# Strassen's scheme in the output projection of a hybrid attention block: chunks 2 and 3 of 4 by seven half-size products for eight

## The reference

```python
mixed = jax.nn.sigmoid(g_sb) * y_sb + jax.nn.sigmoid(g_sa) * y_sa
h = h + jnp.einsum('bsd,de->bse', mixed, w_out[layer])     # (512 x 2048) by (2048 x 2048)
return rms_norm(h, final_norm_gain)
```

## Time and profile before

| | |
|---|---|
| median of three runs | 1643.45 us |
| the profiled execution's own time | 1644.75 us |
| its span (first to last instruction) | 1643.1 us |
| TensorE matmul busy | 1628.2 us, 99% |
| TensorE weight load busy | 1357.3 us, 83% |
| VectorE busy | 754.4 us, 46% |
| ScalarE busy | 580.9 us, 35% |
| GpSimd busy | 16.2 us, 1% |
| moved by DMA | 165.90 MB, mean 101 GB/s |
| granted TensorE clock, mean | 0.998 of full |

### The profile page before, as it was taken

One profiled execution on the slowest core, in us unless ns is written; L12 is line 12 of the kernel. 1 busy time (PEld: TensorE's weight loads), 2 busy tenths in 40 slices (PEclk: granted clock), 3 DMA queues, 4 the chain that ended last, 5 costly groups with the idle time before them and its releaser, 6 DMA issues.

```text
span 1643.1 us, 20351 instructions
## 1 busy us (share of the span) xinstructions
PE 1628.2 (99%) x7443; PEld 1357.3 (83%) x7443; DVE 754.4 (46%) x1116; ACT 580.9 (35%) x926; POOL 16.2 (1%) x37
## 2 busy tenths in 40 slices
PE   8999999999999999999999999999999999999998
PEld 6888888888888888888888888888888888888886
DVE  5334678622125444354544554444455544434333
ACT  5333333222225454344443233333233433313222
POOL 0000000000000000000000000000000000000000
PEclk9999999999999999999999999999999999999999
DMA  5232233333333322233323333323232523253233
GB/s 195 78 100 79 79 89 90 102 89 91 103 102 91 96 83 83 83 98 88 96 77 103 105 93 96 93 85 95 83 102 83 185 90 103 90 202 121 94 106 115
DMA packets 82043, 165.90 MB, mean 101 GB/s; under 512 B 7104, under 2 KB 7632, under 8 KB 80848
## 3 DMA queue, kind: packets, MB, share of 16 engines
q1 hardware_dynamic: 77808, 150.10, 30.1%
q0 software_dynamic: 3040, 13.63, 2.2%
q10 hardware_dynamic: 1152, 1.57, 0.3%
HBM read 156.90 MB, written 8.39 MB: 101 GB/s over the span
## 4 chain that ended last, share of the span: by engine, by line
PE 98%; DMA 0%; DVE 0%; ACT 0%; issue 0%; SPq 0%; DVEq 0%
PE proj L1098 28%; PE proj L1099 28%; PE proj L1100 28%; PE attn L1099 3%; PE attn L1100 3%; PE attn L1098 3%; PE attn L1259 1%; PE attn L1288 1%; PE attn L1220 1%; PE attn L1219 1%; PE attn L1146 0%; DMA xs<-in_x 0%; PE proj L1166 0%; PE attn L1261 0%; DVE xs L738 0%
## 5 line engine op out<-in xcount | busy, mean ns | idle before, releaser
L1098 PE MATMUL proj<-u_hi,w_hi 128*128 128x512 f32 x1536 | 600.9, 391 | 2.5 <-DVE xs L738 2.5
L1099 PE MATMUL proj<-u_lo,w_hi 128*128 128x512 f32 x1536 | 598.7, 390 | 0.0
L1100 PE MATMUL proj<-u_hi,w_lo 128*128 128x512 f32 x1536 | 598.7, 390 | 0.0
L683 DVE TENSOR_TENSOR w_lo<-stage,w_hi 128x1024 fp32r<-128x1024 f32 x267 | 325.9, 1223 | 518.1 <-ACT w_hi L369 515.5
L369 ACT ACTIVATE w_hi<-stage 128x1024 fp32r<-128x1024 f32 x267 | 282.0, 1060 | 484.6 <-PE proj L1100 356.7
L1098 PEld LDWEIGHTS proj<-u_hi,w_hi 128*128 128x128 f32 x1536 | 288.9, 188 | 61.8 <-DVE xs L738 2.8
L1100 PEld LDWEIGHTS proj<-u_hi,w_lo 128*128 128x128 f32 x1536 | 288.7, 188 | 60.4
L1099 PEld LDWEIGHTS proj<-u_lo,w_hi 128*128 128x128 f32 x1536 | 288.9, 188 | 58.4
L385 ACT ACTIVATE area<-proj 128x512 f32 (+1 forms) x80 | 47.9, 599 | 171.3 <-PE proj L1100 171.2
L1098 PE MATMUL proj<-w_hi,u_hi 128*128 128x512 f32 x256 | 99.9, 390 | 0.0
L1100 PE MATMUL proj<-w_hi,u_lo 128*128 128x512 f32 x256 | 99.6, 389 | 0.0
(11 more groups left out here) (177 smaller groups left out, 1419.9 us busy)
## 6 DMA issues: line engine op xcount, KB each, us to landing
stage<-in_w_in SPq DMA_DIRECT2D x208, 512.0 KB, 3.7
stage<-in_w_out SPq DMA_DIRECT2D x32, 512.0 KB, 3.6
stage<-in_w_branch_sb SPq DMA_DIRECT2D x16, 512.0 KB, 3.6
stage<-in_w_branch_sa SPq DMA_DIRECT2D x16, 512.0 KB, 4.0
xs<-in_x SPq DMA_DIRECT2D x4, 1024.0 KB, 8.7
o_scratch<-og POOLq DMA_DIRECT2D x16, 256.0 KB, 2.3
hres<-in_x POOLq DMA_DIRECT2D x1, 4096.0 KB, 13.6
o_in<-o_scratch POOLq DMA_DIRECT2D x3, 1024.0 KB, 6.1
```

Of the source, the lines that this page charges most:

```text
L683: V.tensor_tensor(w_lo[:, s % RING, :, :], stage[:, s % 2, :, :], w_hi[:, s % RING, :, :].bitcast(F), ALU.subtract).then_inc(strip_lo, 1)
L1098: nc.tensor.matmul(out_, a_hi, b_hi, start=start, stop=False, skip_group_check=free)
L1099: nc.tensor.matmul(out_, a_hi, b_lo, start=False, stop=False, skip_group_check=free)
L1100: return nc.tensor.matmul(out_, a_lo, b_hi, start=False, stop=stop, skip_group_check=free)
```

## The change

Chunk 30 stays as it was. Chunks 31 and 32 are computed by the Strassen-Winograd scheme. Tokens are halved (256 and 256), W's K tiles are split into even and odd ones, and the 512 columns into two of 256 (`HW`). Seven products of half size replace eight. A unit of this work is a form strip q = 0 to 15 (eight for each chunk); it holds seven forms of a pair of K tiles, each 128 x 256: B11, B22, B21 and the sums S1 to S4. TensorE runs 7 products x 2 token tiles x 3 = 42 matmuls of 256 moving columns per form strip (`form_strip`).

- SP's queue issues three loads for each form strip into one of four `raw` buffers. Two of them write their source twice, so that S1 and S3 begin as copies.
- GpSimd's queue then adds the missing block to S1 and S3 by a DMA that accumulates (16 of them, line 433 of the new file).
- VectorE adds S2 and S4 (`form_sums`), ScalarE writes the high parts of all seven forms (`form_high`, 1792 columns, three buffers), VectorE the low parts over the raw ones (`form_low`). A `raw` buffer is free again when TensorE is through with its form strip, and only then is form strip q + 4 loaded.
- The left operand's four combinations E7, E5, E6, E3 for each of eight pairs of K tiles are built by VectorE (`e_build`, four operations), split by ScalarE (`e_high`) and VectorE (`e_low`). Pairs 0 to 2 are built in branch chunk 29, 3 to 5 in chunk 30, 6 and 7 behind form strips.
- The seven products of a chunk are put together by VectorE in eleven steps (`blocks`), the first product being copied out by ScalarE.
- The residual is loaded in two parts, the first three quarters (3 MB) when the last of mixed is ready, the last quarter near the end. Chunk 33 takes its W from loads of its own (`last_raw`), freed by form strips 8 to 15.

The core of the diff:

```diff
-            with sp.Fori(C_OUT, C_END) as c:
-                load_chunk(c, rows(wout), c * CW - C_OUT * CW)
+            load_chunk(C_OUT, rows(wout), 0)
+            def load_forms(q):
+                if q < 2:
+                    sp.wait_ge(strip_used, NS * C_OUT + 6)
+                elif q < RAWS:
+                    sp.wait_ge(strip_used, NS * C_OUT + NS)
+                else:
+                    sp.wait_ge(form_used, q - RAWS + 1)
+                k, r = 2 * (q % NS), q % RAWS
+                for kt, part, form, copies in ((k, 1, B11, 2), (k + 1, 0, B22, 2), (k + 1, 1, B21, 1)):
+                    sp.dma_start(raw[r][:, form:form + 3 * copies - 2:3, :],
+                                 wout[:, kt:kt + 1, out_cols(q, part)].to_broadcast([P, copies, HW])
+                                 ).then_inc(form_loaded[r], 16)
...
+            for q in range(FAST):
+                load_forms(q)
+                if q >= 12:
+                    load_last(q - 12)
+            for s in range(4, NS):
+                load_last(s)
...
-            pool.wait_ge(strip_used, NS * C_OUT)
-            pool.dma_start(hres[:, :, :], x[0].rearrange("(i p) d -> p i d", p=P)).then_inc(res_loaded, 16)
+            pool.wait_ge(mix_lo, KT)
+            pool.dma_start(hres[:, :, :], x[0].rearrange("(i p) d -> p i d", p=P)[:, :, 0:3 * CW]).then_inc(res_loaded, 16)
             pool.dma_start(fgain[:, :], final_gain.rearrange("(a d) -> a d", a=1).to_broadcast([P, D_MODEL])
                            ).then_inc(fgain_loaded, 16)
+            for q in range(FAST):
+                r = q % RAWS
+                pool.wait_ge(form_loaded[r], 48 * (q // RAWS + 1))
+                pool.dma_start(raw[r][:, S1:S3 + 1, :],
+                               wout[:, 2 * (q % NS):2 * (q % NS) + 1, out_cols(q, 0)].to_broadcast([P, 2, HW]),
+                               accum_op=ALU.add).then_inc(form_added[r], 16)
...
+            def e_high(p):
+                def f():
+                    act.wait_ge(e_part, 4 * p + 4)
+                    A(e_hi[:, p, :, :], e_raw[:, p, :, :], ACT.Copy).then_inc(e_hi_ready, 1)
+                return f
...
+            def square(m, i):
+                if 4 * m + i:
+                    act.wait_ge(sq_done, 4 * m + i)
+                src = hres_last[:, i, :] if m == 3 else hres[:, i, CW * m:CW * m + CW]
+                A(t_sum[:, :], src, ACT.Square, accum_out=ssq[:, i, m:m + 1]).then_inc(sq_done, 1)
+            def form_high(q):
+                act.wait_ge(form_sum, 2 * q + 2)
+                if q == 0:
+                    act.wait_ge(strip_lo, NS * C_OUT + NS)
+                    act.wait_ge(strip_used, NS * C_OUT + 6)
+                elif q == 1:
+                    act.wait_ge(strip_used, NS * C_OUT + 7)
+                elif q >= HIS:
+                    act.wait_ge(form_used, q - HIS + 1)
+                A(form_hi[q % HIS][:, :, :], raw[q % RAWS][:, :, :], ACT.Copy).then_inc(form_hi_ready, 1)
+            def first_product(m):
+                act.wait_ge(product_done, (FORMS - 1) * m + 1)
+                A(t_sum[:, :], product_bank(m, 0)[:, :], ACT.Copy).then_inc(p1_ready, 1)
...
+            for s in range(LEAD, NS):
+                split_hi(C_OUT, s)
+                if s >= 5:
+                    e_high(s - 2)()
+            for q in range(FAST):
+                form_high(q)
+                if q in (2, 3):
+                    e_high(q + 4)()
+                if q == 3:
+                    for i in range(QT):
+                        act.wait_ge(h_ready, i + 1)
+                        square(0, i)
+                if q == 8:
+                    first_product(0)
+                if q == 11:
+                    act.wait_ge(block_step, BLOCK_STEPS)
+                    for i in range(QT):
+                        square(1, i)
+                if q >= 12:
+                    last_high(q - 12)
...
+            def e_build(p):
+                def f():
+                    if p < 3:
+                        dve.wait_ge(strip_used, NS * (C_OUT - 1) + NS // 2)
+                    else:
+                        dve.wait_ge(strip_used, NS * C_OUT)
+                    dve.wait_ge(mix_lo, 2 * p + 2)
...
+                    V.tensor_tensor(a_raw[:, :, :].rearrange("p (k h) s -> p k (h s)", k=2),
+                                    area_r[:, 4 * p:4 * p + 3:2, :].bitcast(F),
+                                    area_r[:, 4 * p + 1:4 * p + 4:2, :].bitcast(F), ALU.add).then_inc(e_part, 1)
+                    dve.wait_ge(e_part, 4 * p + 1)
+                    V.tensor_tensor(e_raw[:, p, E7:E5 + 1, :], a_raw[:, 0:2, :], a_raw[:, 1:4:2, :],
+                                    ALU.subtract).then_inc(e_part, 1)
+                    dve.wait_ge(e_part, 4 * p + 2)
+                    V.tensor_tensor(e_raw[:, p, E6, :], e_raw[:, p, E5, :], a_raw[:, 0, :],
+                                    ALU.subtract).then_inc(e_part, 1)
+                    dve.wait_ge(e_part, 4 * p + 3)
+                    V.tensor_tensor(e_raw[:, p, E3, :], a_raw[:, 2, :], e_raw[:, p, E6, :], ALU.add).then_inc(e_part, 1)
+                return f
+            def e_low(p):
+                dve.wait_ge(e_hi_ready, p + 1)
+                V.tensor_tensor(e_lo[:, p, :, :], e_raw[:, p, :, :], e_hi[:, p, :, :].bitcast(F),
+                                ALU.subtract).then_inc(e_lo_ready, 1)
...
+            chunk(C_OUT - 1, [None, None, None, None, e_build(0), mix_sb(C_OUT - 1), e_build(1), e_build(2)])
+            mix_both(C_OUT - 1)
+            def form_sums(q):
+                r = q % RAWS
+                dve.wait_ge(form_added[r], 16 * (q // RAWS + 1))
+                V.tensor_tensor(raw[r][:, S2, :], raw[r][:, S3, :], raw[r][:, B11, :], ALU.add).then_inc(form_sum, 1)
+                dve.wait_ge(form_sum, 2 * q + 1)
+                V.tensor_tensor(raw[r][:, S4, :], raw[r][:, S2, :], raw[r][:, B21, :], ALU.add).then_inc(form_sum, 1)
+            def form_low(q):
+                dve.wait_ge(form_hi_ready, q + 1)
+                V.tensor_tensor(form_lo[q % RAWS][:, :, :], raw[q % RAWS][:, :, :],
+                                form_hi[q % HIS][:, :, :].bitcast(F), ALU.subtract).then_inc(form_lo_ready, 1)
...
+            def blocks(m, first, end):
...
+                c11, c21, c12, c22 = block(0, 1), block(1, 1), block(0, 0), block(1, 0)
+                pr = [two(product_bank(m, p)) for p in range(FORMS)]
...
+                steps = [(c11, c11, ts, ALU.add, 0), (ts, pr[1], ts, ALU.add, 2), (us, pr[2], ts, ALU.add, 3),
+                         (c11, pr[3], c11, ALU.add, 4), (c21, pr[4], c21, ALU.add, 5), (c12, pr[5], c12, ALU.add, 6),
+                         (c22, pr[5], c22, ALU.add, 0), (c21, c21, us, ALU.add, 0), (c12, c12, ts, ALU.subtract, 0),
+                         (c22, c22, us, ALU.subtract, 0), (c12, pr[6], c12, ALU.add, 7)]
+                for j in range(first, end):
+                    o_, a, b, op, product = steps[j]
+                    if j == 0:
+                        dve.wait_ge(p1_ready, m + 1)
+                    if product == FORMS:
+                        dve.wait_ge(form_used, NS * (m + 1))
+                    elif product:
+                        dve.wait_ge(product_done, (FORMS - 1) * m + product)
+                    if BLOCK_STEPS * m + j:
+                        dve.wait_ge(block_step, BLOCK_STEPS * m + j)
+                    V.tensor_tensor(o_, a, b, op).then_inc(block_step, 1)
+            for s in range(LEAD, NS):
+                split_lo(C_OUT, s)
+                if s == 2:
+                    for p in range(3):
+                        e_low(p)
+                if s >= 5:
+                    e_build(s - 2)()
+                if s >= 6:
+                    e_low(s - 3)
+            form_sums(0)
+            e_low(5)
+            form_sums(1)
+            form_low(0)
+            dve.wait_ge(res_loaded, 16)
+            dve.wait_ge(fgain_loaded, 16)
+            for i in range(QT):
...
+                bank_done(dve, C_OUT, i)
+                V.tensor_tensor(t, proj[i][:, :], t, ALU.add).then_inc(h_ready, 1)
+            for q in range(FAST):
+                if q + 2 < FAST:
+                    form_sums(q + 2)
+                if q + 1 < FAST:
+                    form_low(q + 1)
+                if q in (1, 2):
+                    e_build(q + 5)()
+                if q in (2, 3):
+                    e_low(q + 4)
+                if q == 4:
+                    times_gain(0)
+                if q == 7:
+                    blocks(0, 0, 8)
+                if q == 8:
+                    blocks(0, 8, BLOCK_STEPS)
+                if q == 15:
+                    blocks(1, 0, BLOCK_STEPS)
+                if q >= 12:
+                    last_low(q - 12)
...
-            with pe.Fori(C_OUT + 1, C_LAST) as c:
-                chunk(c, tokens="mixed")
+            def product_free(m, p):
+                if m == 0:
+                    if p < 4:
```

(44 more changed lines are left out.)

202 lines of the change are left out of this document (122 added, 80 removed).

## The result

The changed kernel takes 1678.21 us (median of 4 runs, 1676.35 to 1679.59) against 1643.49 for the kernel before on the same chip: a ratio of 1.0211, 95% interval 1.0199 to 1.0224. It is 34.7 us slower, where 16.0 had been predicted and 27.5 was the upper end of the range.

A forecast was written before the change was run, and what follows sets the result against it. The prediction took the output projection to be bound by TensorE, busy 40.00 of 40.00 us. Stalls of 19.6 us plus 1.7 for the clock less a 5.3 gain made +16.0, a median of about 1659.5 us, range 1649 to 1671.

The forecast's parts named there:

- item 6: Ring of four raw buffers: reloading, accumulation and sums pace form strips at 5.3 us against 5.1; 1.5 us (0 to 8).
- The term for the clock: TensorE's clock falls to half level once, at the longest stall, costing 1.7 us (0 to 3.4).
- TensorE's gain: Chunks 31 and 32: 224 triples of 256 columns replace 128 of 512, saving 5.3 us (4.2 to 6.4).
- the rival built on 13 ns less: Long runs of 256-column matmuls lose their extra 13 ns each, making it 10 us less: 1650; chance 0.04.
- Item 1: Strip 4 of chunk 30: the later residual load delays the strip's load and low part; 2.0 us (0 to 4).
- Items 2 and 3: Form strips 0 and 1: load, accumulation, sums and low parts come late; 2.0 us (1 to 4) and 3.7 (3 to 5).
- Item 4: Form strip 4: E's pair 7 and four squares stand ahead of its high and low parts; 6.5 us (4 to 8).
- Item 5: Form strip 9: eight block steps on VectorE stand ahead of its sums and low part; 3.9 us (2 to 5).
- the accumulation is slow: Rival: accumulating DMAs take 5 to 6 us and the ring sets the pace, 1665 to 1672; chance 0.14.

The follow-up runs named there:

- h1: Changed kernel with VectorE making all four sums after one load, most E pairs built by GpSimd, and work reordered: 1639.72 us against 1643.01 for the kernel before.
- e4: Changed kernel with one 512 KB load per form strip and four VectorE additions in place of two and an accumulating transfer: 1652.56 us, ratio 1.0056.
- f1: e4 with strip 0's low part first, E pairs 6 and 7 split later, squares spread over strips 5 to 7, gain product behind 10: 1648.05 us.
- e3: Changed kernel with E pairs 3 to 7 all built in chunk 30, squares behind strips 3 to 6, gain product behind 9: 1678.41 us, ratio 1.0219.
- f3: Changed kernel with 12 useless 512-column matmuls ahead of the waits for form strips 4 and 7: 1671.97 us, ratio 1.0172.
- e1: Changed kernel without the sixteen accumulating transfers, so chunks 31 and 32 of the output are not the product: 1651.45 us, ratio 1.0046.
- f2: As e4, but with the four additions made by GpSimd in place of VectorE: 1654.47 us, ratio 1.0069.
- h2: h1 with the changed kernel's loads, accumulating transfers and two VectorE sums: 1667.31 us, ratio 1.0147.

## Why the prediction was wrong

The direction was right, the time 18.7 us too low: the measured 1678.2 lies above the whole range. The step that failed is item 6, the ring of four. It was put at 1.5 us of waits and cost 18.5, for the loop from a used buffer to the next low part takes 13.8 us and not 10.9, with load and accumulation both mis-sized. The term for the clock fell with it, 10.1 us for 1.7. The other items were right or lay too high.

- **TensorE's gain, 5.3 (4.2 to 6.4): right.** Starts are 0.12 apart, and an undisturbed strip takes 5.04 us. h1 shows the stage nearly clear of waits: 83.8 us against 87.0 with 1.9 of waits in it, so 5.1. The 109.2 ns of the Trainium skill ("TensorE: Matmul & The Clock Gate", section Back-to-back issue gap), which the page gives for a single matmul by itself and calls too low for a stream with weight loads at small sizes, and the rival built on 13 ns less don't appear.
- **Item 1, strip 4 of chunk 30, 2.0: absent.** Building E in chunk 29 held up next to nothing: mixed was complete 1.5 us earlier than before, with chunk 30 1.7 earlier. The residual's load went out at 1464.76, not at 1468. The strip's own load, issued 0.9 us behind it (5.9 before), landed in 10.4 us against 11.1, and the high part came at 1476.03, 0.6 us earlier than in the earlier trace rows when counted from the start of the chunk. So a later residual doesn't move the loads behind it by as much as item 1 had it; why, these traces don't say.
- **Items 2 and 3, form strips 0 and 1, 5.7: 5.3 (4.59 and 0.73), but the parts are partly luck.** For strip 0 the load took 5.8 us until GpSimd could go on, for the 4.2 put in, and the accumulation 4.5 for 3.5; that is the 2.6 by which its wait is longer. The chain of strip 1 took 12.9 us for 10.9, yet its wait is small, because strip 0 ran at half clock and took 7.63 us in place of 5.1. The waits of 3 to 4 us that were to stand before strips 1 and 9 aren't there.
- **Item 4, 6.5: 5.28**, by the chain as predicted, 10.6 us long for 11.4. (By its own terms the item comes to 6.3 + 0.6 = 6.9.) ScalarE, then VectorE:

```profile
1530.84 1.06 ACT L721 ACTIVATE e_hi<-e_raw 128x1024 fp32r<-128x1024 f32 x1 [6.91 <-DVE e_raw L1174]
1531.81 0.61 ACT L734 ACTIVATE t_sum<-hres 128x512 f32<-128x512 f32 x1
...
1534.86 3.27 ACT L745 ACTIVATE form_hi<-raw 128x1792 fp32r<-128x1792 f32 x2
```

```profile
1536.58 2.03 DVE L1197 TENSOR_TENSOR form_lo<-raw,form_hi 128x1792 fp32r<-128x1792 f32 x1 [2.85 <-ACT form_hi L745]
```

- **Item 5, strip 9, 3.9: 0.98** in the changed kernel, where strips so far apart leave room for the block steps; 1.56 in e4 and f1.
- **Item 6, the ring of four, 1.5 (0 to 8): 18.5** (strips 3, 7, 10, 11, 13 and 14). The first turn is strip 3, whose low part stands behind the sums of strip 4, the first to use a buffer again:

```profile
1525.20 0.42 DVE L1191 TENSOR_TENSOR raw<-raw 128x256 f32<-128x256 f32 x1 [3.95 <-DMA raw<-in_w_out]
1525.66 0.42 DVE L1193 TENSOR_TENSOR raw<-raw 128x256 f32<-128x256 f32 x1
1526.00 2.02 DVE L1197 TENSOR_TENSOR form_lo<-raw,form_hi 128x1792 fp32r<-128x1792 f32 x1
```

  For strip 7, SP, GpSimd and VectorE show the same:

```profile
1546.11 0.37 SPq L353 DMA_DIRECT2D raw<-in_w_out  x1
```

```profile
1550.92 1.19 POOL L433 DMA_DIRECT2D raw<-in_w_out  x1 [10.52 <-DMA raw<-in_w_out]
```

```profile
1558.60 0.43 DVE L1191 TENSOR_TENSOR raw<-raw 128x256 f32<-128x256 f32 x1 [10.99 <-DMA raw<-in_w_out]
1559.06 0.42 DVE L1193 TENSOR_TENSOR raw<-raw 128x256 f32<-128x256 f32 x1
1559.40 2.02 DVE L1197 TENSOR_TENSOR form_lo<-raw,form_hi 128x1792 fp32r<-128x1792 f32 x1
```

  The load of strip 8 takes 4.8 us, its accumulation 7.7, and the low part of 7 stands behind its sums. The loop was drawn rightly, the durations in it weren't. In the median the time from SP's first issue of a strip to GpSimd's is 5.8 us (4.8 to 8.9): the 4.5 that the experiments reckon with is the third load's alone, which is issued 1 us behind the first. So the loop is 5.8 + 4.8 + 0.9 + 2.0 + 0.3 = 13.8 us beside two strips of 10.2, where I had 10.9. Four turns of 3.6 us are 14.4 of the 18.5. The rest goes with the spread, and the spread has a pattern: the five accumulations behind which SP issued a load within 1.3 us took 5.2 to 8.1 us, the other eleven 4.4 to 5.5 (in e3 5.7 to 7.4 against 4.4 to 5.0). Whether the loads are what slows them no run here tests. I took 3.5 for the accumulation from POOL's 256 KB store (2.3) and 1 MB load (6.1); the size was near, the kind wasn't. That is the rival "the accumulation is slow", whose 1665 to 1672 "more with the clock" came nearest and had 0.14.
- **Clock, one fall, 1.7 (0 to 3.4): five, 10.1.** I took the price of a fall from the earlier trace rows and gave it to the longest stall alone. In f3 less standing still went with less half clock, and h1, with no wait over 1.55 us in the stage, has none. The stalls and the clock aren't separate terms: a slow strip also hides part of the next wait, as strip 1 shows.

## What to carry over

Leaving out one product in eight pays about 5 us of 87 here. In the kernels tried, it paid only where the sums cost the supplying engines' time but no second transfer: with four VectorE additions of 0.42 us and an order laid out by hand it gives 3.3 us, with an accumulating transfer in the chain it costs 24 to 35. (A ring of more than four buffers, which would give the chain more time, wasn't tried.) Where buffers go round a ring, count the whole loop from release to use in measured durations, at the slow end of their spread, and against the ring's depth; average load says nothing of it. The time of a load is to be taken from its first issue to where the next engine goes on, and several issues in a row count. A stall of several us on TensorE should be priced with the clock that it costs. Stalls are best mended one after the other on one base, for one can hide the next (e3).

## What the runs showed of the hardware

- An accumulating GpSimd transfer of 256 KB keeps GpSimd 1.19 us at its issue and lands in 4.4 to 8.1 us, with 5.2 and more where loads were issued right behind it. A plain write of the same blocks lands in 3.7 in the median. Row of the group in the changed kernel's trace:

```profile
L433 POOL DMA_DIRECT2D raw<-in_w_out x16: 1179/1194/1212, 1497.8 to 1607.1; - x16
DMA to landing us min/median/max: 4.4/4.8/8.1
```

- VectorE's 128x1024 subtraction took 1.22 us alone and 2.01 on average beside GpSimd's additions, single ones 3.4; the 256-column sum 0.42 and up to 2.5.
- Half-level stretches of the clock lasted 3.41 or 6.83 us wherever the form stage had one. In the changed kernel the waits of 5.3 and 4.6 us had the longer ones, but in e1 the wait of 5.28 had 3.41, in f3 one of 4.59 too, and in e1 one of 2.14 as well. Waits of 2.6 to 2.8 us stood without any (changed kernel, f2, h2). What decides between them these runs don't tell.
